# Reordering the middle of the token mixers on three engines

## The reference, cut to what matters

```python
def token_mixers(h, st, p, l):
    u = h @ p['w_in'][l]
    xa, ga, xb, zb, xc, gc = jnp.split(u, SPLITS, axis=-1)
    a = xa * jax.nn.sigmoid(ga)
    a, new_buf_a = causal_dwconv(a, buf_a, p['conv_a_w'][l], p['conv_a_b'][l])       # 31 taps
    a_out = jax.nn.silu(group_layernorm(a, p['ln_a_g'][l], p['ln_a_b'][l], G_A))
    cb = jax.nn.silu(causal_dwconv(xb, buf_b, p['conv_b_w'][l], p['conv_b_b'][l])[0])
    q, k, v = headwise(cb, p['w_q'][l]), headwise(cb, p['w_k'][l]) * (DH_B ** -0.5), headwise(xb, p['w_v'][l])
    ...
    hb, C1, n1, m1 = mlstm_chunkwise(q, k, v, ig, lf, C0, n0, m0)
    hb = head_layernorm(hb, p['gn_b_g'][l])
    b_out = jax.nn.sigmoid(zb) * (hb + p['skip_b'][l] * cb)
    hc, hc1 = rglru(causal_dwconv(xc, buf_c, ...)[0], hc0, ...)                      # scan over positions
    c_out = hc * jax.nn.gelu(gc)
    return jnp.concatenate([a_out, b_out, c_out], axis=-1) @ p['w_out'][l], ...
```

## Time and profile before

| | |
|---|---|
| median of 3 runs | 886.99 us (885.26 to 887.64) |
| the profiled execution | 888.6 us, of it 886.9 us of span |
| PE, busy | 853.5 us, 96% of the span |
| DVE, busy | 706.2 us, 80% |
| ACT, busy | 570.7 us, 64% |
| POOL, busy | 50.5 us, 6% |
| mean granted TensorE clock | 0.984 |

### The profile page before, as it was taken

One profiled execution on the slowest core, in us unless ns is written; L12 is line 12 of the kernel. 1 busy time (PEld: TensorE's weight loads), 2 busy tenths in 40 slices (PEclk: granted clock), 3 DMA queues, 4 the chain that ended last, 5 costly groups with the idle time before them and its releaser, 6 DMA issues.

```text
span 886.9 us, 14123 instructions
## 1 busy us (share of the span) xinstructions
PE 853.5 (96%) x5398; PEld 762.6 (86%) x5398; DVE 706.2 (80%) x905; ACT 570.7 (64%) x673; POOL 50.5 (6%) x98
## 2 busy tenths in 40 slices
PE   7997999999999999997999999999999999999996
PEld 7986999999999999977987888888788888888783
DVE  5997978556656438998978988888878889888888
ACT  6549876434444337279846777776777777776763
POOL 2000014000000001010102000000000000000031
PEclk8999899999999999998999999999999999999998
DMA  9920238997355547510455999999999999999992
GB/s 357 393 89 1 66 139 325 396 419 288 119 188 198 191 166 300 210 50 1 156 209 211 347 364 398 350 403 359 372 371 362 389 357 392 365 392 352 371 347 95
DMA packets 40008, 240.74 MB, mean 271 GB/s; under 512 B 5032, under 2 KB 5384, under 8 KB 19328
## 3 DMA queue, kind: packets, MB, share of 16 engines
q1 hardware_dynamic: 32864, 209.09, 62.3%
q0 software_dynamic: 5936, 27.19, 8.0%
q10 hardware_dynamic: 1152, 3.69, 1.0%
HBM read 215.01 MB, written 25.51 MB: 271 GB/s over the span
## 4 chain that ended last, share of the span: by engine, by line
PE 87%; ACT 6%; DVE 4%; issue 1%; DMA 1%; DVEq 0%; SPq 0%; ACTq 0%
PE ps L514 11%; PE ps L515 11%; PE ps L516 11%; PE ps L841 10%; PE ps L843 9%; PE ps L842 9%; PE ps L855 4%; PE ps L857 4%; PE ps L856 4%; PE ps L555 1%; PE ps L863 1%; DVE xtok L1935 1%; PE ps L591 1%; ACT whi L969 1%; PE ps L918 1%
## 5 line engine op out<-in xcount | busy, mean ns | idle before, releaser
L1732 DVE TENSOR_TENSOR low<-raw,whi 128x2048 fp32r<-128x2048 f32 (+1 forms) x144 | 299.9, 2109 | 49.0 <-ACT whi L1224 48.5
L1224 ACT ACTIVATE whi<-raw 128x2048 fp32r<-128x2048 f32 (+1 forms) x144 | 252.8, 1780 | 73.3 <-DMA raw<-in_w_experts 56.6
L969 ACT ACTIVATE whi<-raw 128x2048 fp32r<-128x2048 f32 (+1 forms) x58 | 105.7, 1825 | 107.6 <-PE ps L516 107.5
L338 DVE TENSOR_TENSOR low<-raw,whi 128x2048 fp32r<-128x2048 f32 (+2 forms) x66 | 131.6, 1996 | 41.2 <-ACT whi L969 41.0
L514 PE MATMUL ps<-nhi,whi 128*128 128x264 f32 x528 | 151.5, 287 | 1.8 <-issue 1.1
L515 PE MATMUL ps<-nlo,whi 128*128 128x264 f32 x528 | 150.3, 285 | 0.0
L516 PE MATMUL ps<-nhi,low 128*128 128x264 f32 x528 | 149.7, 283 | 0.0
L841 PE MATMUL ps<-whi,ehi 128*128 128x512 f32 (+1 forms) x384 | 147.0, 383 | 1.3 <-issue 1.1
L843 PE MATMUL ps<-whi,elo 128*128 128x512 f32 (+1 forms) x384 | 144.9, 377 | 0.0
L842 PE MATMUL ps<-low,ehi 128*128 128x512 f32 (+1 forms) x384 | 144.8, 377 | 0.0
L514 PEld LDWEIGHTS ps<-nhi,whi 128*128 128x128 f32 x528 | 99.5, 188 | 3.2 <-issue 1.9
(11 more groups left out here) (405 smaller groups left out, 1381.9 us busy)
## 6 DMA issues: line engine op xcount, KB each, us to landing
raw<-in_w_experts SPq DMA_DIRECT2D x104, 1024.0 KB, 6.9
raw<-in_w_dense SPq DMA_DIRECT2D x53, 1024.0 KB, 5.1
raw<-in_w_experts SPq DMA_DIRECT2D x32, 768.0 KB, 6.0
xs<-zero POOLq DMA_DIRECT2D x5, 2560.0 KB, 34.5
Cs<-in_state_c POOLq DMA_DIRECT2D x2, 2064.0 KB, 10.3
out_new_s<-Cs POOLq DMA_DIRECT2D x2, 2064.0 KB, 8.2
raw<-in_w_dense SPq DMA_DIRECT2D x8, 512.0 KB, 3.6
raw<-in_w_experts SPq DMA_DIRECT2D x8, 512.0 KB, 6.2
```

What stands on the lines that cost most here:

```text
L338: return engine.tensor_tensor(low[:, u % NRAW, part], raw[:, u % NRAW, part], whi[:, u % NHI, part].bitcast(F32), ALU.subtract)
L969: act.activation(whi[:, u % NHI, 0:n], raw[:, u % NRAW, 0:n], ACT.Copy).then_inc(hi_done, 1)
L1224: act.activation(high_slot(odd, c)[:, 0:kt * w], raw[:, c % NRAW, 0:kt * w], ACT.Copy).then_inc(hi_done, 1)
L1732: dve.tensor_tensor(low[:, c % NRAW, part], raw[:, c % NRAW, part], high_slot(odd, c)[:, part].bitcast(F32), ALU.subtract).then_inc(lo_don ...
```

## The change

Nothing that is computed changes; only the order within each engine's stream, a few PSUM banks and two waits. In words:

- PE: the scores come before the turned values and wait for `R_dve` in place of `E_done`; the mean of the layer norm goes to banks 2 and 3 and waits for `P_done`; the first prompt tile's numerators wait for less; the variance follows the numerators, into the same banks; half of z's first unit runs before the factor is brought back, half of z's second unit after it; w_out's first unit is cut into two pairs of planes (`first_out`), each with its own wait.
- ACT: the table of exponential and logarithm is loaded once before the gates, and one load is dropped; `E` is exponentiated ahead of four small exponentials; the square of the layer norm moves ahead of the gates of RG-LRU, its root behind the widening; the head norm's root, a unit's high part, silu and the skip stand ahead of the spreading of the sample states, which moves behind `Cp`.
- DVE: 30 of the 31 taps stand ahead of `gg`, where 26 did; RG-LRU's scan, and the low parts of the sample keys and values, move from ahead of the numerators to behind the head norm.

The diff, cut to its core:

```diff
@@ -123,7 +123,8 @@
-TAPS = (0, 26, 31)
+VA0 = 272
+TAPS = (0, 2, 30, 31)
...
             def mixer_scores(l):
 
-                pe.wait_ge(S["E_done"], l + 1)
+                pe.wait_ge(S["R_dve"], 3 * (l + 1))
                 pe.wait_ge(S["dec_done"], l + 1)
                 for h in range(H):
                     pe.matmul(ps[:, h, 0:TP], kT[:, h, 0:P], qT[:, h, 0:TP], start=True, stop=True)
@@ -661,19 +662,18 @@
             def lna_mean(l):
 
                 pe.wait_ge(S["conv_a_done"], 3 * (l + 1))
-                pe.wait_ge(S["v1_done"], 3 * l + 2)
+                pe.wait_ge(S["P_done"], l + 1)
                 for i in range(2):
-                    last = pe.matmul(bank(4 + i, T), gmean[:, :], ac[:, i, :], start=True, stop=True)
+                    last = pe.matmul(bank(2 + i, T), gmean[:, :], ac[:, i, :], start=True, stop=True)
                 last.then_inc(S["lna_ps"], 1)
 
             def lna_variance(l):
 
                 pe.wait_ge(S["lna_sq"], l + 1)
-                pe.wait_ge(S["P_done"], l + 1)
                 for j, (t0, n) in enumerate(TILES):
                     for i in range(2):
-                        c = 4 * j + 2 * i
-                        last = pe.matmul(ps[0:n, j // 2, c:c + 2], sga[:, i, t0:t0 + n], gmean[:, 0:P:64],
+                        c = VA0 + 4 * j + 2 * i
+                        last = pe.matmul(ps[0:n, 2 + j // 2, c:c + 2], sga[:, i, t0:t0 + n], gmean[:, 0:P:64],
                                          start=(j != 1 and i == 0), stop=(j > 0 and i == 1))
                 last.then_inc(S["lna_ps"], 1)
 
@@ -688,13 +688,13 @@
 
             def mixer_numerator(l):
 
-                pe.wait_ge(S["lna_xm"], l + 1)
-                pe.wait_ge(S["v1_done"], 3 * (l + 1))
-                pe.wait_ge(S["nq_out"], l + 1)
                 pe.wait_ge(S["P_done"], l + 1)
+                pe.wait_ge(S["v1_done"], 3 * l + 2)
                 for h in range(H):
                     o = slice((h % 2) * (P + 1), (h % 2 + 1) * (P + 1))
                     pe.matmul(ps[:, 4 + h // 2, o], E[:, h, 0:P], v1[:, 0, h, :], start=True, stop=True)
+                pe.wait_ge(S["v1_done"], 3 * (l + 1))
+                pe.wait_ge(S["nq_out"], l + 1)
                 for h in range(H):
                     o = slice((h % 2) * (P + 1), (h % 2 + 1) * (P + 1))
                     pe.matmul(ps[:, 6 + h // 2, o], E[:, h, P:TP], v1[:, 0, h, :], start=True, stop=False)
@@ -734,28 +734,46 @@
                     last = pe.matmul(bank(b + h, ROUND[r] * (P + 2)), ks[0:ROWS, h * P:(h + 1) * P], spread_rows(r)[:, :, h, :], start=True, stop=True)
                 last.then_inc(S["outer_ps"], 1)
 
+            def first_out(l):
+
+                G = 20 * l + 4
+                u, (_, _, _, w, ks) = FIRST_UNIT[G], GROUPS[G]
+                pe.wait_ge(free[0], freed(G) - 1)
+                split_ready(u)
+                hi, lo = unit(whi, u, 4, w), unit(low, u, 4, w)
+                for pair in range(2):
+                    pe.wait_ge(S["y_hi"], 3 * l + pair + 1)
+                    pe.wait_ge(S["y_lo"], 3 * l + pair + 1)
+                    for i in range(w // P):
+                        o, c = bank(i, T), slice(i * P, (i + 1) * P)
+                        for k in (2 * pair, 2 * pair + 1):
+                            kx = ks[0][k]
+                            pe.matmul(o, hi[:, k, c], nhi[:, kx, :], start=(k == 0), stop=False)
+                            pe.matmul(o, hi[:, k, c], nlo[:, kx, :], start=False, stop=False)
+                            last = pe.matmul(o, lo[:, k, c], nhi[:, kx, :], start=False, stop=False)
+                last.then_inc(used, 1)
+
             def mixers(l):
                 mixer_gates(l)
                 mixer_products(l)
                 mixer_broadcast(l)
                 mixer_keys_turned(l)
                 sample_queries(l)
+                mixer_scores(l)
                 mixer_values_turned(l)
-                mixer_scores(l)
                 lna_mean(l)
+                mixer_numerator(l)
                 lna_variance(l)
-                mixer_numerator(l)
+                group(20 * l + 3, nhi, nlo, (0,), (0, 1))
                 lna_back(l)
-                group(20 * l + 3, nhi, nlo, (0,), (0, 1))
+                group(20 * l + 3, nhi, nlo, (1,), (0, 1))
                 pe.wait_ge(S["lna_done"], l + 1)
                 group(20 * l + 3, nhi, nlo, (0,), (2, 3))
-                group(20 * l + 3, nhi, nlo, (1,))
+                group(20 * l + 3, nhi, nlo, (1,), (2, 3))
                 mixer_turn_back(l)
                 mixer_prompt_state(l)
 
-                pe.wait_ge(S["y_hi"], 3 * l + 2)
-                pe.wait_ge(S["y_lo"], 3 * l + 2)
-                group(20 * l + 4, nhi, nlo, (0,))
+                first_out(l)
...
                 hi(U + 3)
+                hi(U + 4)
                 act.wait_ge(S["ga_in"], l + 1)
                 act.activation(sga[:, :, :], sga[:, :, :], ACT.Sigmoid).then_inc(S["sga_done"], 1)
-                hi(U + 4)
                 act.wait_ge(S["mix_w"], 16 * MIX_DMAS * (l + 1))
...
-                act.preload_act_table(ACT.Exp)
+                act.preload_act_table_set("natural_log_exp_and_others")
...
                 act.activation(rows[:, 2, :], rows[:, 2, :], ACT.Ln, bias=1.0).then_inc(S["gate_ln"], 1)
-                act.preload_act_table(ACT.Exp)
 
                 act.wait_ge(S["k_ps"], l + 1)
                 act.activation(kT[:, :, :], ps[:, 4:8, 0:T], ACT.Copy, scale=float(P) ** -0.5).then_inc(S["k_out"], 1)
+                act.preload_act_table(ACT.Exp)
...
+                act.wait_ge(S["R_dve"], 3 * (l + 1))
+                act.activation(dec[:, :, 0, :], ps[:, 0:4, TP:T], ACT.Exp).then_inc(S["dec_done"], 1)
                 act.wait_ge(S["ct_dve"], 3 * (l + 1))
+                for h in range(H):
+                    act.activation(E[:, h, 0:TP], E[:, h, 0:TP], ACT.Exp, bias=cols[:, 0, 0, h:h + 1])
+                    last = act.activation(E[:, h, TP:384], E[:, h, TP:384], ACT.Exp, bias=cols[:, 1, 0, h:h + 1])
+                last.then_inc(S["E_done"], 1)
...
+                act.wait_ge(S["lna_xm"], l + 1)
+                act.activation(sga[:, :, :], ac[:, :, :], ACT.Square).then_inc(S["lna_sq"], 1)
...
+                act.wait_ge(S["rg_dve"], l + 1)
+                act.activation(tmp, tmp, ACT.Sqrt, scale=0.25).then_inc(S["rg_sqrt"], 1)
...
+                act.wait_ge(S["var_done"], l + 1)
+                act.activation(hr[:, :, :], hr[:, :, :], ACT.Sqrt, bias=LN_EPS).then_inc(S["sd_done"], 1)
+                act.preload_act_table(ACT.Silu)
+                hi(U + 8)
                 act.activation(vs[64:64 + NB, :, 0:P + 1], v1[0:NB, 2, :, :], ACT.Copy).then_inc(S["split_hi"], 1)
                 act.activation(ks[32:32 + NB, :], ktok[0:NB, 2, :], ACT.Copy).then_inc(S["split_hi"], 1)
-                hi(U + 8)
...
-                act.wait_ge(S["split_hi"], 4 * (l + 1))
-                act.wait_ge(S["split_lo"], 2 * l + 1)
-                spread(0)
-                decay(0, (0, 1))
-                act.wait_ge(S["var_done"], l + 1)
-                act.activation(hr[:, :, :], hr[:, :, :], ACT.Sqrt, bias=LN_EPS).then_inc(S["sd_done"], 1)
-                act.preload_act_table(ACT.Silu)
                 act.wait_ge(S["lna_done"], l + 1)
                 for i in range(2):
                     last = act.activation(ac[:, i, :], ac[:, i, :], ACT.Silu, scale=A_(l, 32, i), bias=A_(l, 33, i))
@@ -1172,17 +1186,21 @@
                 for h in range(H):
                     last = act.activation(cb[:, h, :], cb[:, h, :], ACT.Copy, scale=B_(l, 6, h))
                 last.then_inc(S["sk_done"], 1)
+                decay(0, (0, 1))
                 act.wait_ge(used, U + 8)
                 act.wait_ge(S["y_f32"], l + 1)
                 act.activation(nhi[:, 0:2, :], ac[:, :, :], ACT.Copy).then_inc(S["y_hi"], 1)
+                act.wait_ge(free[0], freed(20 * l + 3))
+                act.activation(vT[:, :, :], vT[:, :, :], ACT.Tanh, scale=0.5).then_inc(S["sz_done"], 1)
                 act.wait_ge(S["rg_done"], l + 1)
                 act.activation(nhi[:, 6:8, :], gg[:, :, :], ACT.Copy).then_inc(S["y_hi"], 1)
                 hi(U + 9)
-                act.wait_ge(free[0], freed(20 * l + 3))
-                act.activation(vT[:, :, :], vT[:, :, :], ACT.Tanh, scale=0.5).then_inc(S["sz_done"], 1)
                 act.wait_ge(S["cp_ps"], l + 1)
                 act.wait_ge(S["h_norm"], l + 1)
                 act.activation(Cp[:, :, :], ps[:, 4:8, T:T + P + 1], ACT.Copy).then_inc(S["cp_out"], 1)
+                act.wait_ge(S["split_hi"], 4 * (l + 1))
+                act.wait_ge(S["split_lo"], 2 * l + 1)
+                spread(0)
                 decay(0, (2, 3))
...
-                dve.wait_ge(used, U + 4)
-                scaled(xbp[:, :, 3:3 + T], 4, 4).then_inc(free[1], 1)
                 conv_a_taps(0)
+                dve.wait_ge(used, U + 4)
```

(26 more changed lines are left out.)

59 lines of the change are left out of this document (16 added, 43 removed).

## The result

The changed kernel takes 895.71 us (median of 9 runs, 891.78 to 898.33), the one before 888.78 us (median of 9, 885.26 to 889.89): ratio 1.0079, 95% interval 1.0063 to 1.0096, so 6.9 us slower. The forecast was 6.0 us slower, with a range from 4.4 us faster to 9.5 us slower. The profiled execution has a span of 894.0 us against 886.9, 7.1 us more.

A forecast was written before the change was run, and what follows sets the result against it. PE's gaps cost 8.0 us a layer, but the chain through ACT and DVE to `yb` stands close behind. Layers lose 3.2 and 2.9 us: +6.1 on the profiled 888.6, 893.0 against the median; range 882.6 to 896.5.

The forecast's parts named there:

- Waits of PE that would not come back: PE's gaps at scores and variance, with the clock 8.0 us a layer; only 2.4 us of it reaches ACT.
- The front: Taps ahead of `gg`: `gg` 2.45 and 1.63 us later, the values 1.5 us late in layer 0, 0.7 in layer 1.
- The middle: Turned keys to `yb`: root 5.0 us earlier, then 9.2 us on ACT, 11.4 on DVE; `yb` +1.5 and +0.7 us.
- The gap and the clock: PE waits 3.8 us for `yb` at the outer products; the clock falls, costing 2.2 us a layer.
- the 0.5 for `xl`: Layer 0: 0.5 us that PE waited for `xl` before, taken off the loss of 3.7 us.
- rival D: Gaps of 1.0 and 1.3 us at w_out's first unit lower the clock: about 896 us; D and E together 0.07.
- Rival B: Clock holds in the new gap at the outer products: 888.7 to 889.2 us; chance 0.19.
- E: Variance still waits, its square waiting for the mean; old gap beside the new, about 898 us; D and E together 0.07.
- Rival C: ACT's copies and unit fit its waits, `nhi` starts when z ends at 102.7: 882.6 us; chance 0.20.
- The sum: Layer 0 +3.2 us, layer 1 +2.9, together +6.1 on the profiled 888.6; 893.0 us against the median.
- the scan on DVE: RG-LRU's scan with its two neighbours, 2.1 us, now in DVE's chain between `nhi` and `yb`.
- the moved work on ACT: Sample copies and a unit's high part (3.12 us) and a decay (1.85) moved between root and `nhi`: 5.0 us.

The follow-up runs named there:

- the filled gap in the kernel before: Kernel before with 16 unneeded products added on PE between the layer norm's mean and variance, plus a wait for their bank: 887.97 us, ratio 0.9988.
- the gap filled: Changed kernel with 26 unneeded products added on PE ahead of the outer products of round 0: 891.13 us, ratio 1.0022.
- scan early: Changed kernel with RG-LRU's scan and its gate product moved ahead of the low part of planes 0 and 1 on DVE: 885.91 us, ratio 0.9961.
- copies late: Changed kernel with ACT's two copies of sample values and keys and the first decay moved behind the tanh of z: 889.28 us, ratio 1.0021.
- the change again: The changed kernel itself, unaltered, run for a second trace: 896.70 us, ratio 1.0128 to the kernel before.
- taps back: Changed kernel with the eight tap instructions returned behind `gg`, `xbp` staying behind the first two taps: 892.82 us, ratio 1.0031.
- scan late alone: Kernel before with only RG-LRU's scan and its gate product moved behind the low part of planes 0 and 1: 899.68 us, ratio 1.0138.
- taps alone: Kernel before with only the taps of the change, `xbp` behind the first two and 30 of 31 ahead of `gg`: 890.08 us, then 892.07.
- with the taps back: Changed kernel with RG-LRU's scan moved early on DVE and the eight tap instructions returned behind `gg`: 884.24 us, ratio 0.9944.
- second unit's low part late: Changed kernel with scan early and taps returned, plus the low part of w_out's second unit moved behind `yb` on DVE: 882.30 us, ratio 0.9942.

## Why the prediction was right

The range, 882.6 to 896.5, reaches to both sides of the kernel before, so a time inside it says little. What was put to the test is the direction (slower, given 0.60), the 6 us, and the mechanism behind them.

**Waits of PE that would not come back.** Right. Both gaps went, and a chain through ACT and DVE took their place; the filled gap in the kernel before shows it on its own (0.9 us of 2.8 reached `yb`).

**The front.** Right, in size too: `gg` 0.88 + 1.36 = 2.24 us later (forecast 2.45), the values 0.25 + 1.36 = 1.6 (1.9), the gates of C 1.28 (1.5). The copy of the queries does hold the values up, but only for the last 0.20 us. Most of the delay was already there: the keys' products ahead of them waited 0.98 us for ACT's `rows`, which follow `gg` through the gelu. The prediction named that path through ACT for the keys' copy and the gates of C, not for the keys' products. The dropped table load was costed at nothing: ACT waits 1.82 us for the keys' products right behind the gates, more than the 1.28 us of a load. That is a reading; no run put the load back.

**The middle.** Right. From ACT's root to `nhi` of planes 0 and 1: 105.33 - 96.15 = 9.18 us (9.2). DVE from there to `yb`: 117.59 - 105.96 = 11.6 us (11.4). The waits at the two low parts were 2.10 and 0.71 us. ACT's root came 4.2 us earlier, not 5.0, and `yb` 2.4 us later in layer 0 and 1.7 in layer 1 where I had 1.5 and 0.7. What was missing is a term for the stretch at the lower level in the front: the sample queries' products took 3.13 us in place of 1.93, and ACT then waited 0.97 us for the turned values. By the yardstick of the result it costs 1.2 us, and both layers of the first trace have it. Without it the way from `gg` to `yb` is 1.0 us shorter than before in layer 0 and 0.9 in layer 1; the forecast has 2.45 - 1.5 and 1.63 - 0.7, which is 0.95 and 0.93. With `gg` 2.24 and 1.42 us later, `yb` would be 1.2 and 0.5 us later. What brings that stretch on is open: in layer 0 four of the seven traces with the eight taps ahead of `gg` have it and none of the six without, but in layer 1 it comes in eight of the thirteen, with the taps in either place.

**The gap and the clock.** Right. PE waited 3.49 us (3.8), and the clock was low from 119.2 to 126.05. With the gap filled it stayed up in both layers, so idle time there is what brings it down. The price, taken as 2.2 us a layer, was 1.9 and 1.7 us by the filled gap; from `yb` to the dense block 2.0 us were added in layer 0 (1.7 forecast, with the 0.5 for `xl` off), and from `yb` to the end 2.35 in layer 1. The first two waits in w_out's first unit, 0.51 and 1.09 us (1.0 and 1.3), did not bring the clock down, so rival D did not happen. Rival B did not either, and E did not, since the wait for the variance is gone. Rival C did not, and the run that put `nhi` at the end of z took 889.28 us, not C's 882.6: `yb` gained 1.5 and 0.9 us by it, and PE's gap, which C had under a microsecond, stayed at 3.49.

**The sum.** 3.2 and 2.9 us were forecast for the layers, 4.4 and 4.1 came. The two stretches in the front are 2.4 of that, and without them the sum is the forecast's 6.1. In the first trace the shorter low stretch at the start hid 1.4 of the 8.5. Both are the clock's and differ between executions, so that the medians, 6.9 us apart, come within a microsecond of the 6.0 of the forecast is in part luck; the mechanism does not rest on it.

**What the prediction left open.** It named the scan on DVE and the moved work on ACT together. The runs weigh them: the scan's place costs 9.8 us (taken back) or 11.2 (alone), the copies and the decay on ACT 6.4, the taps about 2 to 3. These are not additive, because the first two share one wait of DVE. The low parts of the sample values and keys, 1.4 us that the change also put into DVE's chain, were not moved back by any run. With the scan and the taps put back, what is left of the change gains 4 to 5 us. So most of the order on PE and ACT was worth having, and above all one DVE block in the wrong place turned it into a loss.

## What to carry to other kernels

When PE's gap is to be closed, look up who has the next thing PE needs after the gap, and how much that engine's chain gives way: a gap is worth only the slack behind it. Work moved out of the way on one engine has to land in a wait of that engine that the same trace shows, here DVE's 2.1 us ahead of the low part of planes 0 and 1, and not behind it; and it has to fit, as ACT's 3.1 us in a wait of 2.6 show. And when the clock falls behind a gap, a filled gap measures its price, apart from the chain.

## What was not expected of the hardware

The stretches at the lower clock level were about 3.4 or 6.8 us long in every trace, apart from one at the very end of the span, and the same code showed different ones: at the start 6.8 us (before) or 3.4 us (the change) or none (scan early, copies late, the change again), and near 74 us in layer 0 3.4 us in one trace of the changed kernel and none in the other. PE was busy there in every half microsecond from 68 us on, in both traces. Such a stretch cost 1.2 us in the front and up to 2.1 us at the start, so single traces of this kernel differ by a good part of the change in question, and two timelines have to be aligned before they are compared. The root at the start serves for that where both traces had a low stretch there. In the second trace of the change, which had none, DVE then waited 0.45 us for ACT, and `gg` started only 0.14 us earlier although the root came 0.73 earlier; so the way from `gg` is the safer measure.

Gaps of 3.5 us at the outer products, with a second of 0.7 to 1.4 us behind them, were followed by 6.8 us at the lower level in eight layers out of eight (the change twice, taps back, copies and decay late). The old gap of 3.9 us at the variance was followed by 6.8 us in seven layers and by 3.4 in one (before, scan late alone, taps alone twice). Gaps of 1.46 and 1.41 us in succession were followed by 3.4 us in three layers and 6.8 in one (scan early, without and with the taps back); a gap of 2.0 us by 3.4 in one layer and by none in the other (second unit's low part late); gaps of 0.51 and 1.09 us, in the changed kernel, by none.
